# Expert weights in a ring of eight 16 KB blocks instead of two sets of three buffers

## The reference

```python
h = x + W_out [ PoolMix(u) ; RMSNorm_head(GLA(q, k, v, alpha)) * silu(r) ]   # [u,q,k,v,r,z] = RMSNorm(x) @ W_in
hn = rmsnorm(h, norm_ffn)
# top-1 of 4 groups, then top-2 of its 8 experts: 32 experts, 2 picks for each token
for e in range(32):                       # rows of hn that picked e
    y = (silu(rows @ w_eg[e]) * (rows @ w_eu[e])) @ w_ed[e]   # 1024x512, 1024x512, 512x1024
h = h + gate * y ; out = rmsnorm(h, norm_final)
```

## Time and profile before

| What | Value |
| --- | --- |
| Median of 3 runs | 1048.99 us (1047.72 to 1050.06) |
| The profiled execution's own time | 1047.59 us |
| Its span in the trace | 1045.7 us |
| PE matmul busy | 994.2 us, 95% |
| PE weight load busy | 788.2 us, 75% |
| DVE, ACT, POOL busy | 561.9, 243.9, 106.1 us |
| DMA | 263.23 MB, mean 252 GB/s |
| Chain that ended last | PE 66%, DMA 28%, DVE 4% |
| TensorE clock granted over the span | 0.994 of full speed |

### The profile page before, as it was taken

How to read it: one execution, slowest core, us unless ns; L and a number is a source line. 1 busy time by engine, 2 the same in 40 slices (tenths; PEclk the granted TensorE clock), 3 DMA queues, 4 the chain that set the end, 5 groups by cost and what they waited for, 6 DMA issues and landing times.

```text
span 1045.7 us, 33186 instructions
## 1 busy us (share of the span) xinstructions
PE 994.2 (95%) x14570; PEld 788.2 (75%) x14570; DVE 561.9 (54%) x1283; ACT 243.9 (23%) x531; POOL 106.1 (10%) x169
## 2 busy tenths in 40 slices
PE   7999999999999999999989999999999999999976
PEld 7786868686867677748778888788787787878842
DVE  2333534444444444427976766665756657566337
ACT  2352332323232323121111111111011110111125
POOL 0110101010101010101111011011011110111000
PEclk9999999999999999999999999999999999999989
DMA  9911010100000101175999999999999999999959
GB/s 328 337 72 41 1 41 0 40 0 40 0 40 0 40 0 40 35 328 179 410 418 424 417 425 419 420 421 416 426 415 419 421 415 424 415 419 420 384 189 387
DMA packets 54293, 263.23 MB, mean 252 GB/s; under 512 B 11368, under 2 KB 13992, under 8 KB 46026
## 3 DMA queue, kind: packets, MB, share of 16 engines
q1 hardware_dynamic: 43466, 235.12, 55.2%
q0 software_dynamic: 8192, 18.06, 4.5%
q10 hardware_dynamic: 2592, 9.44, 2.2%
HBM read 247.11 MB, written 27.19 MB: 262 GB/s over the span
## 4 chain that ended last, share of the span: by engine, by line
PE 66%; DMA 28%; DVE 4%; issue 1%; ACT 1%; SPq 0%; DVEq 0%; POOLq 0%; ACTq 0%
DMA arena<-in_w_ed 23%; PE bank L1422 19%; PE bank L1543 11%; PE bank L1713 11%; PE bank L1725 6%; PE bank L1474 6%; PE bank L1732 4%; DMA arena<-in_w_eg 3%; PE bank L1403 2%; PE bank L1523 1%; DVE hnT L1207 1%; DMA arena<-in_w_in 1%; PE bank L1481 1%; PE bank L1540 1%; PE bank L1802 1%
## 5 line engine op out<-in xcount | busy, mean ns | idle before, releaser
L1422 PE MATMUL bank<-xnT,arena 128*128 128x128 f32 x1728 | 201.1, 277 | 3.4 <-DMA arena<-in_w_in 2.0
L1422 PEld LDWEIGHTS bank<-xnT,arena 128*128 128x128 f32 x1728 | 196.9, 193 | 5.8 <-DVE sA L950 3.5
L1713 PEld LDWEIGHTS bank<-xnT,arena 128*64 128x64 f32 x4096 | 156.7, 137 | 10.9 <-DMA arena<-in_w_eg 7.0
L1713 PEld LDWEIGHTS bank<-hnT,arena 128*64 128x64 f32 x4096 | 156.3, 137 | 9.4 <-issue 5.2
L1713 PE MATMUL bank<-xnT,arena 128*64 128x88 f32 x4096 | 160.2, 240 | 3.2 <-DMA arena<-in_w_eg 1.9
L1713 PE MATMUL bank<-hnT,arena 128*64 128x88 f32 x4096 | 159.3, 239 | 2.3 <-DVE hnT L1216 1.6
L1543 PE MATMUL bank<-arena,mixT 128*128 128x512 f32 x256 | 111.7, 593 | 0.0
L1725 PE MATMUL bank<-arena,osq 128*32 128x384 f32 (+1 forms) x768 | 85.7, 487 | 14.4 <-DMA arena<-in_w_ed 12.3
L1237 DVE TENSOR_SCALAR mixT<-mixT 128x352 f32<-128x352 f32 x32 | 12.4, 388 | 147.5 <-ACT mixT L804 147.5
L1725 PE MATMUL bank<-arena,silu_r 128*32 128x384 f32 (+1 forms) x768 | 85.7, 487 | 6.2 <-DMA arena<-in_w_ed 4.2
L1543 PEld LDWEIGHTS bank<-arena,mixT 128*128 128x128 f32 x256 | 47.9, 190 | 57.2 <-issue 57.1
(11 more groups left out here) (260 smaller groups left out, 999.4 us busy)
## 6 DMA issues: line engine op xcount, KB each, us to landing
arena<-in_w_eg SPq DMA_DIRECT2D x32, 2048.0 KB, 26.9
arena<-in_w_eu SPq DMA_DIRECT2D x32, 2048.0 KB, 27.1
arena<-in_w_ed SPq DMA_DIRECT2D x32, 2048.0 KB, 26.7
hn_rows<-hs ACTq DMA_DIRECT2D x18, 512.0 KB, 3.4
arena<-pick_rows SPq DMA_DIRECT2D x18, 512.0 KB, 10.1
arena<-in_w_in SPq DMA_DIRECT2D x3, 2048.0 KB, 12.8
arena<-in_w_out SPq DMA_DIRECT2D x1, 4096.0 KB, 13.8
out_y_prompt<-arena SPq DMA_DIRECT2D x8, 512.0 KB, 6.2
```

The costliest lines, as they stand in the source:

```text
L1422: last = mm(out, w_in_sb[:, k, a:b], xnT[:, k, :], start=k == 0, stop=k == KD - 1)
L1713: last = mm(out[q * SW:(q + 1) * SW, n * BLOCK:(n + 1) * BLOCK], w[:, k, m * P + q * SW:m * P + (q + 1) * SW], rowsT[b][:, k, :], start=k ...
```

## The change

The weights of the experts are 96 pieces of 2 MB, numbered 3e + kind (gate, up, down). Piece n goes to block n mod 8 of a ring, `ring = blocks 0, 1, 2, 3, 4, 6, 5, 7`. Six blocks are `arena`, the seventh (`work`) and eighth (`late[:, D:]`) are new tensors that the mixer's own work tensors (`one_dv`, `w_pool_sb`, `qk`, `q_wide`, `sc`, `gate_work`, `w_r_sb` and others) are carved from. To free them, `pool_out` moves to `hs`, `is_e`, `own_x`, `over` and `first_sel` move to spent constants, and `own_x` is computed in two parts (18 and 7 of 25).

```diff
-        starts = {("g", 0): 0, ("u", 0): EW, ("d", 0): 2 * EW, ("g", 1): 3 * EW, ("u", 1): KD * D_IN, ("d", 1): KD * D_IN + EW}
+        arena = sb("arena", [P, 6 * EW])
+        work = sb("work", [P, EW])
+        late = sb("late", [P, D + EW])
+        blocks = [arena[:, n * EW:(n + 1) * EW] for n in range(6)] + [work[:, :], late[:, D:]]
+        ring = [blocks[n] for n in (0, 1, 2, 3, 4, 6, 5, 7)]
+        MIXER_LOADS = [1, 1, 1, 1, 1, 0, 1, 0]
+        AROUND = RING
+        def place(b, kind):
+            return divmod(KINDS * b + kind, RING)
...
-            sp.dma_start(w_out_sb, w_out.rearrange("(k p) n -> p k n", p=P)).then_inc(s["w_out_in"], 16)
+            for h in range(2):
+                sp.dma_start(w_out_sb[:, h, :, :], ...[:, :, h * 512:(h + 1) * 512]).then_inc(piece_in[(4, 6)[h]], 16)
...
+            def load_freed(t, b):
+                e = AROUND * t + b
+                if not (isinstance(t, int) and e < 3):
+                    sp.wait_ge(s["pe_u2"], 2 * (e - 2))
+                    load_piece(t, b, 0)
+                    sp.wait_ge(s["pe_d"], e - 2)
+                    load_piece(t, b, 1)
+                sp.wait_ge(s["pe_g"], e - 1)
+                load_piece(t, b, 2)
+
+            sp.wait_ge(s["pe_qk"], TILES)
+            load_piece(0, 0, 0)
+            sp.wait_ge(s["pe_u"], TILES)
+            load_piece(0, 0, 1)
+            sp.wait_ge(s["pe_r"], TILES)
+            load_piece(0, 0, 2)
             sp.wait_ge(s["pe_v"], TILES)
-            load_weights(0, 0)
-            load_weights(0, 1)
+            load_piece(0, 1, 0)
             sp.wait_ge(s["sA_ready"], TILES)
             for p in range(PAIRS):
...
+            sp.wait_ge(s["pe_half_out"], 1)
+            load_piece(0, 1, 1)
+            sp.wait_ge(s["own_rstd_ready"], 1)
+            load_piece(0, 1, 2)
+            sp.wait_ge(s["pe_half_out"], 2)
+            load_piece(0, 2, 0)
+            sp.wait_ge(s["pe_router"], TILES)
+            sp.wait_ge(s["states_stored"], 16 * 2 * PAIRS)
+            load_piece(0, 2, 1)
             sp.wait_ge(s["pool_out_ready"], 2)
...
-            with sp.Fori(1, NE // 2) as t:
-                for b in range(2):
-                    sp.wait_ge(s["pe_g"], 2 * t + b - 1)
-                    load_weights(t, b)
+            for b in range(2, AROUND):
+                load_freed(0, b)
+            with sp.Fori(1, NE // AROUND) as t:
+                for b in range(AROUND):
+                    load_freed(t, b)
@@ scalar
             expert(0, 0, True)
+            act.wait_ge(s["pool_stored"], 16 * 2)
             expert(0, 1, True)
@@ vector
             dve.wait_ge(s["pe_small_T"], 1)
+            dve.wait_ge(s["hn_stored"], 16 * PICKS * TILES)
             for n in range(2):
                 V.tensor_copy(pool_out[n], bank[4 + 2 * n][0:HIST, :]).then_inc(s["pool_out_ready"], 1)
...
-                st(V.tensor_tensor(own_x[:, :, :], con("iota_x")...to_broadcast([P, EXTRA, NE]), ...))
-                st(V.tensor_reduce(x_of[:, :], own_x[:, :, :], AX.X, ALU.add))
+                for a in range(0, EXTRA, X_PART):
+                    n = min(X_PART, EXTRA - a)
+                    st(V.tensor_tensor(own_x[:, 0:n, :], con("iota_x")[:, a:a + n]...to_broadcast([P, n, NE]), ...))
+                    st(V.tensor_reduce(x_of[:, a:a + n], own_x[:, 0:n, :], AX.X, ALU.add))
@@ tensor
-            expert(0, 0)
-            expert(0, 1)
-            with pe.Fori(1, NE // 2 - 1) as t:
-                expert(t, 0)
-                expert(t, 1)
-            expert(NE // 2 - 1, 0)
-            expert(NE // 2 - 1, 1, last=True)
+            for b in range(AROUND):
+                expert(0, b)
+            with pe.Fori(1, NE // AROUND) as t:
+                for b in range(AROUND):
+                    expert(t, b)
```

More of the change, by code:

```diff
@@ L206, in o_of, with carve, by_k, weights @@
             return o_bank[r][:, 0:PAIRS * P].rearrange("p (a n) -> p a n", a=PAIRS)
-        arena = sb("arena", [P, KD * D_IN + KD * D])
-        w_in_sb = arena[:, 0:KD * D_IN].rearrange("p (k n) -> p k n", k=KD)
-        w_out_sb = arena[:, KD * D_IN:KD * D_IN + KD * D].rearrange("p (k n) -> p k n", k=KD)
         EW = KD * FF
-        starts = {("g", 0): 0, ("u", 0): EW, ("d", 0): 2 * EW, ("g", 1): 3 * EW, ("u", 1): KD * D_IN, ("d", 1): KD * D_IN + EW}
-        wg = [arena[:, starts["g", b]:starts["g", b] + EW].rearrange("p (k n) -> p k n", k=KD) for b in range(2)]
-        wu = [arena[:, starts["u", b]:starts["u", b] + EW].rearrange("p (k n) -> p k n", k=KD) for b in range(2)]
-        wd = [arena[:, starts["d", b]:starts["d", b] + EW].rearrange("p (k n) -> p k n", k=KF) for b in range(2)]
+        arena = sb("arena", [P, 6 * EW])
+        work = sb("work", [P, EW])
+        late = sb("late", [P, D + EW])
+        late_at = [3 * NG * (HIST + P)]
+        def carve(n):
+            a = late_at[0]
+            late_at[0] += n
+            assert late_at[0] <= D + EW
+            return late[:, a:a + n]
+        blocks = [arena[:, n * EW:(n + 1) * EW] for n in range(6)] + [work[:, :], late[:, D:]]
+        def by_k(block):
+            return block.rearrange("p (k n) -> p k n", k=KD)
+        w_qk_sb, w_u_sb, w_r_in_sb, w_v_sb = (by_k(blocks[n]) for n in range(4))
+        w_out_sb = arena[:, 4 * EW:].rearrange("p (h k n) -> p h k n", h=2, k=KD)
+        w_z_sb = sb("w_z_sb", [P, KD, P // 4])
+        ring = [blocks[n] for n in (0, 1, 2, 3, 4, 6, 5, 7)]
+        RING = len(ring)
+        KINDS = 3
+        MIXER_LOADS = [1, 1, 1, 1, 1, 0, 1, 0]
+        AROUND = RING
+        def place(b, kind):
+            return divmod(KINDS * b + kind, RING)
+        def weights(b, kind):
+            return ring[place(b, kind)[1]].rearrange("p (k n) -> p k n", k=KF if kind == 2 else KD)
         cst = sb("cst", [P, N_CONST])
@@ L223, in build, with part @@
         ident = con("ident")
-        one_dv = sb("one_dv", [P, P])
+        work_at = [0]
+        def part(n):
+            a = work_at[0]
+            work_at[0] += n
+            assert work_at[0] <= EW
+            return work[:, a:a + n]
+        one_dv = part(P)
         eps = sb("eps", [P, 1])
@@ L279, in build @@
         hs = sb("hs", [P, KD, P])
+        pool_out = [hs[0:HIST, 4 * n:4 * n + 4, :].rearrange("p k n -> p (k n)") for n in range(2)]
         hss = sb("hss", [P, 1])
@@ L378, in build @@
         s = {n: sem(n) for n in names}
[L379 to L381 removed]
+        piece_in = [sem(f"piece_in{n}") for n in range(RING)]
         rows_in = [sem(f"rows_in{b}") for b in range(2)]
@@ L452, in _ @@
                 for p in range(PAIRS):
[L453 to L469, removed]
+                    sp.dma_start(gla_sample[2 * p:2 * p + 2].rearrange("h k v -> (h k) v"), s_sample[:, p, :]).then_inc(s["states_stored"], 16)
@@ new lines, in _ @@
+            load_piece(0, 1, 1)
[6 more added lines that the diff above has]
+            load_piece(0, 2, 1)
+            sp.wait_ge(s["pool_out_ready"], 2)
+            for n, out in enumerate((pool_sample, pool_prompt)):
+                sp.dma_start(out, pool_out[n]).then_inc(s["pool_stored"], 16)
@@ L1417, in turn_x, with features @@
                     last.then_inc(s["pe_xT"], 1)
-            def features(out, a, b):
+            def features(n, w, m):
                 for k in range(KD):
-                    last = mm(out, w_in_sb[:, k, a:b], xnT[:, k, :], start=k == 0, stop=k == KD - 1)
+                    last = mm(bank[n][:, m * P:(m + 1) * P], w[:, k, m * P:(m + 1) * P], xnT[:, k, :], start=k == 0, stop=k == KD - 1)
                 return last
@@ L1542, in out_step @@
             def out_step(n, k, out, mix):
-                return mm(out[:, :], mix[:, k, :], w_out_sb[:, k, n * 512:(n + 1) * 512], start=k == 0, stop=k == KD - 1)
+                return mm(out[:, :], mix[:, k, :], w_out_sb[:, n, k, :], start=k == 0, stop=k == KD - 1)
             def project_out(j):
@@ L1743, in down, with expert, loaded @@
                 return last
-            def expert(t, b, last=False):
-                e = 2 * t + b
+            def expert(t, b):
+                e = AROUND * t + b
+                odd = b % 2
                 first = isinstance(e, int) and e == 0
+                def loaded(kind):
+                    lap, n = place(b, kind)
+                    pe.wait_ge(piece_in[n], 16 * KINDS * t + 16 * (lap + 1 + MIXER_LOADS[n]))
                 pe.wait_ge(s["eT_ready"], 1 if first else 2 * e + 2)
-                pe.wait_ge(g_in[b], 16 * t + 16)
-                up(bank[2 + b], wg[b], b, first=first).then_inc(s["pe_g"], 1)
-                pe.wait_ge(u_in[b], 16 * t + 16)
+                loaded(0)
+                up(bank[2 + odd], weights(b, 0), odd, first=first).then_inc(s["pe_g"], 1)
+                loaded(1)
                 if first:
@@ L1754, in expert @@
                 for half in range(2):
-                    up(bank[4 + half], wu[b], b, HALVES[half]).then_inc(s["pe_u2"], 1)
-                pe.wait_ge(d_in[b], 16 * t + 16)
```

(15 more changed lines are left out.)

129 lines of the change are left out of this document (69 added, 60 removed).

## The result

The changed kernel takes 1085.3 us (median, 1083.13 to 1085.72) against 1048.84 us beside it: ratio 1.0343, 95% interval 1.0325 to 1.0361. It is slower by 36 us where 9 to 10 us of gain were forecast, and 32 us beyond the upper end of the range. The profiled execution took 1085.72 us with a span of 1083.9 us.

The account below looks back on a forecast made before the run. PE bounds first, later the DMA. The DMA's sum, 981 + 2.5 + 4.0 = 987.5 against 996.8, saves 9.3 us and outlasts PE's own account of 990.0: 1038.3 us profiled, 1039.5 forecast, range 1030 to 1053.

Parts of the forecast that it names:

- the price of code loading: PE's eight-expert loop body is fetched anew: 66 more code packets, adding 4.0 us to the DMA's sum.
- the DMA account: Last weights land at 981, plus 2.5 us waiting for free blocks and 4.0 for code: 987.5 against 996.8.
- The jumps back: PE's two jumps to the start of its expert loop stall 3.5 us each.
- Slower, by PE: Rival: start shift d plus two jump stalls S exceed 25 us; d = 12, S = 9 gives 1053; chance 0.11.
- The first gather: Before expert 0, beside pieces 5 to 7, it takes 9.5 us, not 3.9, shifting everything on PE by 5.6.
- The stores of the last rows: DVE's new wait for the last tile's stored rows, before `pool_out`, stays hidden even if they take 12 us.
- The pieces landed before the experts: Eight weight pieces land by about 498; the other 88 at 5.49 us each end at 981, 16 us earlier.
- PE in gaps at experts 16 and 24 much over 4 us: Sign that the forecast is wrong: PE idles much over 4 us at the experts after its two jumps.
- A DMA time per piece over 5.6 us: Sign that the forecast is wrong: weight pieces take longer than 5.6 us each, against the 5.49 assumed.
- DMA share below 0.95 between 510 and 980: Sign that the forecast is wrong: the DMA is not kept full while the experts run.
- The DMA behind it: Expected sign in the chain of waits: PE alone until about expert 26, then the DMA.
- The rival of one DMA engine: All PE code comes over one of 16 DMA engines, 2.4 us more per expert: some 1100 us; chance 0.05.

Follow-up runs that it names:

- The twin kernels: Changed kernel cut to six blocks, differing only in PE's and SP's loop body: two experts 1054.43 us (1.0050), eight experts 1084.41 us (1.0333).
- the old kernel with a long body: Kernel before the change, loads and blocks untouched, with PE's expert code as eight written out and a loop over eight: 1072.7 us, ratio 1.0222.
- the half loads: Changed kernel with each weight load from expert 8 on cut to half its rows, PE's code and waits the same: 1053.83 us, ratio 1.0052.
- The six-block kernel with two in its body: Changed kernel with a ring of six blocks, no third expert loaded ahead, and two experts in PE's loop body: 1054.43 us, ratio 1.0050.
- four experts in the body: Changed kernel with a ring of six blocks and four experts in PE's loop body: 1094.87 us, ratio 1.0456.

## Why the prediction was wrong, step by step

- **The failed step is the price of code loading.** The prediction wrote "66 more, spread over 16 engines that are all busy, are 66 x 0.96 / 16 = 4.0 us", all on the DMA account. The count was right: 98 packets expected, 103 came. Whether the DMA's 4.0 us were right no run shows. But PE's account got nothing for straight code, and PE, not the DMA, must have the packet: 1.19 us for each expert, 32.0 us in all. The twin kernels (30 us for the body's length, same loads), the old kernel with a long body (23 us) and the half loads (experts 15.2 us apart at a share of 0.70) show it. The sum asked what the packets cost the DMA, and not what their lateness costs the engine that reads them.
- **The jumps back** were put at 3.5 us each on the ground of the quickest transfers in the earlier trace rows. They cost 8.8 and 8.0 us over their neighbours: a jump stalls not once but three times, and the granted clock falls after the first stall (0.75 in 768 to 772). The rival "Slower, by PE" named this and allowed d + 2S, with no term for every expert. With d = 14.0 and 2S = 16.7 it stands at 30.7 against the 25 of slack: 6 us slower by itself, and the 32.0 us beside it are the rest of the 37.8.
- **The first gather** was right at 9.5 us (9.47). What followed from it was not: "+5.6" became +9.4 at expert 0. PE idled 5.48 us for it, and when it went on its granted clock stood at the 1.2 GHz level; the 16 matmuls of L1744 and 16 of L1753 ran at that. By expert 4 the shift was 14.0. The six-block kernel with two in its body loses nearly as much with one load in place of three (8.9 us at expert 0), so the landing behind one load, 6.6, was no good lower bound for this one.
- **The stores of the last rows** took 11.0 us after 3.6, inside the bound of 12. They had landed by 491.2, before DVE's row numbers let the second gather go (496.38), so they added nothing.
- **The DMA account** (981 + 2.5 + 4.0) assumed that the DMA never waits for a free block by more than 2.5 us. No run shows that term by itself; the DMA's share of 0.92 in 497 to 553 leaves 56 x 0.08 = 4.5 us in the first stretch alone. In the sum it no longer matters: PE is late, most weights land 11 to 16 us after issue (the page's medians; 27 before), and PE never waits for them.
- **The pieces landed before the experts**: nearly right. 4.3 MB more had come by 497 and the eighth piece landed at 500.4. PE, which was then late, could not use them.
- **Signs.** "PE in gaps at experts 16 and 24 much over 4 us" came: 7.7 us of stalls at expert 16, 6.4 at expert 24. "A DMA time per piece over 5.6 us" came too: 88 pieces from 500.4 to the last landing at 1011.5 are 5.81 us each, since the loads waited for PE's blocks. "DMA share below 0.95 between 510 and 980" did not: it is 0.99 there, and only the stretch to 553 has 0.94. "The DMA behind it" from expert 26 on never came.
- **The rival of one DMA engine** is out: weight loads land sooner after their issue than before, and PE never waits for one in 567 to 990.

The shift grew by another 4.7 us from expert 0 to expert 4, and the trace places most of it. Expert 0's gate and up products took 10.66 us in place of 9.88, with the clock at its lower level until 497. In expert 2 PE waited 2.60 us for DVE (1.57 before), and the down product then ran from 542.58 to 550.67, 8.1 us in place of 5.4, at a granted clock of 0.52 (541 to 548). The waits for code in these experts are 1.9 us, against 1.4 before. Still open is why straight code stalls less with four experts in the body than with eight.

## What to carry to other kernels

Count the instructions of a loop body for each engine before its period is set by a buffer scheme: a body that was resident and is no longer makes PE run at the pace of its code packets when the DMA is full, and costs longer stalls at each jump. A lead in loaded data is worth only what the engine behind it can use; price a late code packet, or a small gather that the first compute waits for, on that engine, with the slow clock after the wait. When DMA time stands free just ahead of a critical small transfer, let the large loads wait for the small one.

## What was not expected of the hardware

- The same number of code packets costs PE 32 us in straight code beside transfers at 400 GB/s, and next to nothing there at 227 GB/s (share 0.70).
- One 2 MB load beside a gather that took 3.9 us alone makes it 8.3, three make it 9.5.
- An idle stretch of 5.48 us on PE was followed by about 9 us of work at the 1.2 GHz level (until 497); the granted clock fell to it after the stalls of 4.46 and 4.50 us at the jumps too. Windows of the kernel after:

```profile
486.00:490.00 4.00, 2.49 (x13) 2.52 (x14) 0.31 (x2) 0.00 (x0) 0.00 (x0) 0.58 1.05 438
490.00:494.00 4.00, 4.00 (x21) 4.00 (x20) 2.07 (x10) 0.00 (x0) 0.00 (x0) 0.50 1.04 441
494.00:498.00 4.00, 4.00 (x60) 3.94 (x61) 2.40 (x8) 0.00 (x0) 1.31 (x2) 0.64 0.98 414
```
